# Down weights loaded as four neighbouring rows per partition, with column tiles that stream every fourth column of the gate and up weights

## The reference

```python
def moe_swiglu(h, router_w, wg, wu, wd):
    t = h.reshape(-1, dm)
    logits = (t @ router_w).astype(jnp.float32)
    top_val, top_idx = lax.top_k(logits, TOP_K)          # 2 of 8
    gates = jax.nn.softmax(top_val, axis=-1)
    combine = jnp.sum(jax.nn.one_hot(top_idx, N_EXPERTS) * gates[..., None], axis=1)
    out = jnp.zeros_like(t)
    for e in range(N_EXPERTS):
        he = jax.nn.silu(t @ wg[e]) * (t @ wu[e])        # wg, wu: 1024 x 3584
        out = out + (combine[:, e:e + 1] * he) @ wd[e]   # wd: 3584 x 1024
    return out
```

## Time and profile before

| | us |
|---|---|
| median of 3 runs (lowest, highest) | 2564.65 (2563.71, 2566.11) |
| the profiled execution | 2566.54 |
| its span, first to last instruction | 2564.8 |
| TensorE busy with matmuls | 2414.3 |
| L755, gate/up matmuls of the first mixture, busy | 590.6 |
| L770, its down matmuls, busy | 300.5 |

### The profile page before, as it was taken

The page is one execution under the profiler, slowest core; times in us unless marked ns, Lnnn a source line. Parts: engine busy times, 40 slices in busy tenths (PEclk is TensorE's granted clock), DMA queues, the critical chain, the costliest instruction groups (busy, mean ns, idle before and its releaser), DMA issues.

```text
span 2564.8 us, 52222 instructions
## 1 busy us (share of the span) xinstructions
PE 2414.3 (94%) x24282; PEld 1574.9 (61%) x24282; DVE 644.9 (25%) x1217; ACT 355.7 (14%) x566; POOL 157.3 (6%) x145
## 2 busy tenths in 40 slices
PE   7979998999999999999999889899999699999996
PEld 5647776756666665666666679895778444444443
DVE  1640002201011110101010366742543322222223
ACT  2220101100000000000000333213242100000001
POOL 2000000000000000000000024520220100000000
PEclk9989999999999999999999889999999799999998
DMA  8693424699999999999999100022123589999994
GB/s 313 224 333 133 143 103 145 227 393 369 393 368 393 369 371 393 370 393 369 393 370 385 58 1 1 1 99 99 66 99 109 198 321 398 399 399 399 399 399 185
DMA packets 274312, 678.53 MB, mean 265 GB/s; under 512 B 5907, under 2 KB 9454, under 8 KB 269870
## 3 DMA queue, kind: packets, MB, share of 16 engines
q1 hardware_dynamic: 271664, 669.01, 69.5%
q0 software_dynamic: 2112, 6.04, 0.7%
q10 hardware_dynamic: 318, 0.10, 0.0%
HBM read 674.08 MB, written 1.05 MB: 263 GB/s over the span
## 4 chain that ended last, share of the span: by engine, by line
PE 72%; DMA 9%; SPq 8%; DVE 7%; ACT 3%; issue 1%; DVEq 0%; ACTq 0%; POOLq 0%
PE ps L656 22%; PE ps L755 20%; PE ps L770 9%; SPq L607 6%; DMA ring<-in_moe_wd 5%; PE ps L840 4%; PE ps L1036 3%; PE ps L855 2%; DMA ring<-in_w_exp_up 2%; ACT arena L2142 2%; PE ps L828 1%; SPq L519 1%; PE ps L1178 1%; PE ps L1341 1%; PE ps L1346 1%
## 5 line engine op out<-in xcount | busy, mean ns | idle before, releaser
L755 PE MATMUL ps<-ring,arena 128*32 128x256 f32 x10752 | 590.6, 379 | 1.1 <-DVE arena L1814 1.1
L755 PEld LDWEIGHTS ps<-ring,arena 128*32 128x32 f32 x10752 | 348.0, 110 | 233.7 <-issue 2.7
L656 PE MATMUL ps<-hT,ring 128*128 128x256 f32 (+1 forms) x1728 | 417.8, 402 | 10.4 <-issue 6.8
L656 PEld LDWEIGHTS ps<-hT,ring 128*128 128x128 f32 x1728 | 335.2, 195 | 95.9 <-issue 49.1
L2142 ACT ACTIVATE arena<-ps 128x256 f32<-128x256 f32 (+4 forms) x254 | 135.3, 558 | 1759.4 <-PE ps L755 781.6
L770 PE MATMUL ps<-ring,arena 128*32 128x256 f32 x5376 | 300.5, 379 | 1.7 <-DMA ring<-in_moe_wd 1.6
L770 PEld LDWEIGHTS ps<-ring,arena 128*32 128x32 f32 x5376 | 173.7, 110 | 117.8 <-DMA ring<-in_moe_wd 3.4
L840 PE MATMUL ps<-ring,arena 128*64 128x512 f32 x768 | 171.6, 601 | 15.6 <-DMA ring<-in_w_exp_up 12.8
L1531 DVE TENSOR_TENSOR arena<-arena,ps 128x384 f32<-128x384 f32 x56 | 31.0, 554 | 586.4 <-ACT arena L2142 586.4
L656 PE MATMUL ps<-arena 128*128 128x128 f32 (+1 forms) x1064 | 130.8, 283 | 11.0 <-DVE arena L1572 3.6
L656 PEld LDWEIGHTS ps<-arena 128*128 128x128 f32 x1064 | 126.5, 198 | 16.0 <-ACT arena L2142 3.8
(11 more groups left out here) (365 smaller groups left out, 1967.1 us busy)
## 6 DMA issues: line engine op xcount, KB each, us to landing
ring<-in_moe_wg SPq DMA_DIRECT2D x56, 2048.0 KB, 12.5
ring<-in_moe_wu SPq DMA_DIRECT2D x56, 2048.0 KB, 17.5
ring<-in_moe_wd SPq DMA_DIRECT2D x56, 2048.0 KB, 19.0
ring<-in_w_exp_gate SPq DMA_DIRECT2D x24, 2048.0 KB, 23.1
ring<-in_w_exp_up SPq DMA_DIRECT2D x24, 2048.0 KB, 19.9
ring<-in_w_exp_down SPq DMA_DIRECT2D x24, 2048.0 KB, 18.8
ring<-in_w_in SPq DMA_DIRECT2D x14, 2048.0 KB, 9.2
ring<-in_w_ada SPq DMA_DIRECT2D x12, 2048.0 KB, 13.5
```

The lines of the kernel that those rows point to most:

```text
L656: last = mm(outp, l, r, start=(i == 0), stop=(i == n - 1))
L755: last = mm(o_, x_[:, k, 32 * r:32 * r + 32], gu[:, :, k, :, q, :], start=(k == 0), stop=(k == KC - 1))
```

## The change

The down weights of the first mixture are loaded with four neighbouring rows in each partition in place of rows 128 apart. With that, the hidden column at (c, q, i) has to be 128q + 4i + c, so the view of the gate and up weights that `up` streams from is written with `c` innermost. All else stays, `down` and the second mixture too.

```diff
@@ -516,7 +516,8 @@
                     s_ = 3 * (w % 2) + t
                     name, k = (("moe_wg", KC), ("moe_wu", KC), ("moe_wd", 4))[t]
                     src = ins[name][0][e, :, j * UW:(j + 1) * UW] if t < 2 else ins[name][0][e, j * UW:(j + 1) * UW, :]
-                    sp.dma_start(ring[:, s_, :].rearrange("p (k n) -> p k n", k=k), src.rearrange("(k p) n -> p k n", p=P))\
+                    rows_ = "(k p) n -> p k n" if t < 2 else "(p k) n -> p k n"
+                    sp.dma_start(ring[:, s_, :].rearrange("p (k n) -> p k n", k=k), src.rearrange(rows_, p=P))\
                         .then_inc(inc("%sloaded%d" % ("" if x == "m" else "x1_", s_)), 16)
@@ -747,7 +748,7 @@
                         for s_ in (3 * par, 3 * par + 1):
                             pe.wait_ge(*at("%sloaded%d" % (ld, s_), (ld0 + h0 + w // 2) * 16 + 16))
-                        gu = ring[:, 3 * par:3 * par + 2, :].rearrange("p m (k c q i) -> p m k c q i", k=KC, c=4, q=4)
+                        gu = ring[:, 3 * par:3 * par + 2, :].rearrange("p m (k q i c) -> p m k c q i", k=KC, q=4, c=4)
                         for r in range(3):
                             for k in range(KC):
                                 for q in range(4):
```

## The result

The changed kernel takes 3211.05 us (median of 4 runs, 3208.06 to 3213.86), the one before 2564.22 us beside it: a ratio of 1.2518, 95% interval 1.2498 to 1.2538, so 646.8 us slower. The forecast of 2562.5 us was wrong. The time lies inside the wide range and in case C (3145 us, 2700 to 3900), to which the prediction gave 0.13.

The account below looks back on a forecast made before the run. The prediction took TensorE to set the pace, with the DMA close behind. From 2564.65 us it took 2.1 for the down step's waits and added 0 for the strided gate/up stream: 2562.5 us, range 2560 to 4545.

Parts of the forecast that it names:

- case C: Gate/up matmuls: a strided stream runs at half pace, +581 us, 3145 us (2700 to 3900); chance 0.13.
- What bounds the kernel: First mixture: TensorE sets the pace, DMA close behind; TensorE waits 1.6 us for weights, the SP queue 449.8 us for buffers.
- Case E: Whole kernel faster by over 0.2%: DMA is the true bound, its savings worth up to 40 us, 2525 us; chance 0.05.
- The 0.7 us less for a down transfer: Down-weight loads: 16 KB pieces may take about 4.8 us of DMA time in place of 5.5.
- Part (1): Down-weight loading in `fetch`: only TensorE's waits at the down step are saved, 2.1 us, between nothing and 2.6.
- Part (2): Moving operand in `up`, read at a 16-byte step: point 0 us, bounds from nothing to +1978 us.
- The moving stream needs a float every 0.84 ns only: Gate/up matmuls: the stream's need, set against strided reads priced at 0.83 to 0.93 ns a float.
- the free end: Gate/up matmuls: strided streaming costs nothing, a group of four stays at 0.216 us; chosen for the point.
- L846's strided load: Transpose load at a 16-byte step, the nearest row: 202 ns, read as 0.93 ns a float against 0.45 contiguous.
- case B: Gate/up matmuls: each strided stream pays by itself, +59 us, 2624 us (2575 to 2700); chance 0.20.
- Case D: Gate/up matmuls: four strided streams share one reader, 0.850 or 0.952 us a group, 4269 to 4543 us; chance 0.29.
- VectorE's row (L2072): VectorE writing 256 results at 256-byte steps, 628 ns against 480 contiguous for another operation; cited for a price on steps.

Follow-up runs that it names:

- e1: Changed kernel with gate/up weights streamed contiguously as before, only the new down-weight loading kept: 2563.93 us against 2565.73 before, ratio 0.9993.
- e8: Kernel before, with loaded tokens and odd gathers' loads at various steps, and shorter moving runs: 32-column load 136 ns at step 4, 110 contiguous.
- e5: Kernel before, each expert's gate/up matmuls reading at another step from 1 to 16 floats: 0.216 us a group at step 1, 0.457 at step 4.
- e7: Kernel before, each expert's gate/up matmuls reading pairs, fours or other run lengths: 0.227 us a group for pairs every 4 floats, 0.456 at step 4.
- e6: Kernel before, a group's four matmuls on four, two or one tiles, at various steps: on one tile 0.216 us a matmul at step 1, 0.452 at step 4.
- e3: Changed kernel streaming 128 neighbouring columns per tile, with VectorE's multiply writing the permuted order: 2564.76 us against 2565.73 before, ratio 0.9996.
- e9: Changed kernel streaming 128 neighbouring columns per tile, with TensorE writing PSUM at a step of 32 floats: 2564.66 us against 2564.57 before, ratio 0.9995.

## Why the prediction was wrong

- What bounds the kernel: right. TensorE's steps set the pace, so nearly all of L756's added time went to the total. Case E is out by e1. The 0.7 us less for a down transfer is shown by no run: in the stretch that the text reads as 419 to 446 GB/s the row has 400 to 465 and behind it 341 to 413, and e1 moves 383 GB/s against 381. Only case E rested on it.
- Part (1), 2.1 us between nothing and 2.6: right. In e1 L771's wait is gone and the mixture is 2.2 us shorter; the total time is too coarse to show it.
- Part (2) held the failure. The step of it that failed is "The moving stream needs a float every 0.84 ns only", and with it the choice of the free end. It took L846's strided load, 0.93 ns a float, for the pace of any strided read of TensorE, an absolute floor just under the need of the stream. Even so 0.93 lies above 0.84, and its own middle bound, case B, would have made 59 us of it; the point took nothing. The stream needed 1.78 ns a float, and a group 0.454 us. What carries over from that row is the ratio: the transposed load went from 0.45 to 0.93, the ordinary load goes from 0.83 to 1.64 (e8), the moving stream from 0.84 to 1.78 (e5 to e7). That the ratio is what carries over is seen in these three, not explained. The row stood in the text, as case C, with that very ratio, and was given 0.13.
- The rule of the Trainium skill that the prediction weighed ("Advanced Engine Details and Errata", "Memory Cachelines") held: a new line for every element pays, two hits per line nearly hide it (0.228 against 0.216 us at step 2). The price in these runs is 1.78 ns a piece. The forecast set it aside on the strength of the misread row.
- Case C's own sum, 581 us, was 66 short, of which 2688 x (0.454 - 2 x 0.216) = 59 us is the price above the double: 1.78 ns a piece, not 1.69. Why it is not the round double wasn't found; the DMA's writes and the clock are excluded by the windows above. That the time lies in case C is the case's mechanism and not luck; that it lies in the whole range of 2560 to 4545 us says little, as four different mechanisms fill it.
- Case D, which had 0.29, rested on a count of bytes that fitted one 16-byte read per 0.84 ns. With its own prices it was out with the result (0.454 us a group, not 0.85 or more), and with reads of 0.44 ns it fell in e6.
- VectorE's row (L2072) gave no size for TensorE, but its direction was right, for VectorE as well: e3's write at a step of 128 bytes costs 0.29 us for 384 results, 0.76 ns each.

## What to carry to other kernels

When the same work must be laid out for two users, put the step where nothing waits for it: TensorE's write to PSUM (free here) or VectorE's write (0.29 us, hidden), not the operand that TensorE streams, where a step of four floats doubles the matmul however many tiles share the array. In runs of 32 floats and more, two floats per 16 bytes keep nearly all of the pace: a step of two floats costs 6%, one of three 58%; in runs of 4 a step of two costs 16 to 20%. A price read from a neighbouring row was here better carried over as a ratio to its own contiguous form than as an absolute time, and where TensorE sets the pace, an edit to the DMA's pieces was worth no more than the waits that TensorE had for it (2.2 us).

## What the runs showed that was not expected

- TensorE wrote PSUM in single floats 128 bytes apart at its full pace: 10.38 us a step in e9.
- In e8 the granted clock fell from 1.00 to 0.50 (1.2 GHz) in the gathers with strided loads (a step of eight floats). The rows are e8's windows. TensorE was busy all the time by its records, but with a 128-column load every 0.24 us and matmuls of 96 columns between them. The contiguous gathers of the same kernel kept 1.00. The fall did not lengthen the gather: at the pace of its first 14 loads, all at 1.00, 32 take 32 x 0.244 = 7.8 us, as measured, and the windows have 10 matmuls in 2 us at 1.00 and 14 in 3 us at 0.65. It did cost behind it: the transposes at 0.50, whose loads are contiguous, took 1.49 us for 0.82.

```profile
703.50:708.00 4.50, 4.45 (x42) 4.21 (x38) 0.58 (x2) 0.01 (x1) 0.00 (x0) 1.00 1.03 396
...
822.00:824.00 2.00, 2.00 (x10) 2.00 (x10) 0.00 (x0) 0.00 (x0) 0.00 (x0) 1.00 1.03 393
824.00:827.00 3.00, 3.00 (x14) 3.00 (x14) 0.00 (x0) 0.00 (x0) 0.00 (x0) 0.65 1.05 388
827.60:829.00 1.40, 1.40 (x8) 1.13 (x7) 0.00 (x0) 0.00 (x0) 0.00 (x0) 0.50 1.06 389
```
